# Decoder layer with grouped experts: the first blocks' preparations put in another order, and each expert's weights loaded in six pieces instead of three

## What is computed

```python
def expert_block(args):
    e, x_blk = args
    hidden = jax.nn.silu(x_blk @ exp_w_gate[e]) * (x_blk @ exp_w_up[e])
    return hidden @ exp_w_down[e]
...
x = x + hybrid_mixer(h, w_in[l], ..., w_out[l])
h = rmsnorm(x, ln2_g[l])
x = x + hierarchical_moe(h, ...)      # 32 experts, 2 for each token
return rmsnorm(x, ln_f_g)
```

## Time and profile before

| what | value |
|---|---|
| times of three runs | 1393.38, 1395.4, 1390.2 us; median 1393.38 |
| the profiled execution's own time | 1391.23 us |
| its span (first to last instruction) | 1389.6 us |
| PE busy | 1217.4 us, 88% |
| DVE busy | 884.1 us, 64% |
| ACT busy | 737.6 us, 53% |
| HBM read, written | 245.52 MB, 25.79 MB |
| `mix_and_route` ends, `experts` begins | about 726 us |
| `experts` ends, `finish` begins | about 1364 us |

### The profile page before, as it was taken

How to read it: one execution, slowest core, us unless ns; L and a number is a source line. 1 busy time by engine, 2 the same in 40 slices (tenths; PEclk the granted TensorE clock), 3 DMA queues, 4 the chain that set the end, 5 groups by cost and what they waited for, 6 DMA issues and landing times. The chain is left out here.

```text
span 1389.6 us, 17581 instructions
## 1 busy us (share of the span) xinstructions
PE 1217.4 (88%) x6516; PEld 949.5 (68%) x6516; DVE 884.1 (64%) x823; ACT 737.6 (53%) x756; POOL 269.6 (19%) x268
## 2 busy tenths in 40 slices
PE   3999999898899988699935999999999999999990
PEld 2867677676688768388824777777777777777760
DVE  5155554646366348334566788888888888887853
ACT  6154545545343243312224777776778777677643
POOL 0000000000201002000063343343333243233330
PEclk9999999999999995599967999999999999999995
DMA  5210101000111020163219899999999999999927
GB/s 166 61 31 16 31 16 31 15 17 1 46 46 31 1 90 32 46 234 121 92 42 372 308 366 369 362 355 359 364 358 360 365 359 354 359 351 354 358 70 265
DMA packets 69807, 263.22 MB, mean 189 GB/s; under 512 B 12944, under 2 KB 46848, under 8 KB 57472
## 3 DMA queue, kind: packets, MB, share of 16 engines
q1 hardware_dynamic: 60880, 245.69, 47.8%
q0 software_dynamic: 8880, 16.88, 5.3%
HBM read 245.52 MB, written 25.79 MB: 195 GB/s over the span
## 5 line engine op out<-in xcount | busy, mean ns | idle before, releaser
L1814 PE MATMUL ps<-w_high,x_hi 128*128 128x512 f32 x512 | 206.7, 404 | 3.3 <-DVE x_lo L1735 3.3
L1814 PE MATMUL ps<-w_high,x_lo 128*128 128x512 f32 x512 | 203.7, 398 | 0.0
L1814 PE MATMUL ps<-w_lower,x_hi 128*128 128x512 f32 x512 | 203.5, 397 | 0.0
L1731 DVE TENSOR_TENSOR w_lower<-w_raw,w_high 128x2048 fp32r<-128x2048 f32 x64 | 143.7, 2287 | 45.0 <-ACT w_high L1660 45.0
L1660 ACT ACTIVATE w_high<-w_raw 128x2048 fp32r<-128x2048 f32 x62 | 115.8, 1908 | 85.9 <-DMA w_raw<-exp_w_up 82.0
L1726 DVE TENSOR_TENSOR w_lower<-w_raw,w_high 128x2048 fp32r<-128x2048 f32 x62 | 141.6, 2284 | 24.7 <-ACT w_high L1654 24.7
L1590 POOL DMA_INDIRECT y_dram<-y,where x32 | 86.6, 2706 | 359.4 <-ACT y L1685 359.4
L1754 DVE TENSOR_TENSOR d_lo<-cat,d_hi 128x2048 fp32r<-128x2048 f32 x64 | 145.1, 2284 | 17.5 <-ACT d_hi L1675 17.4
L420 DVE TENSOR_TENSOR_SCAN prod<-stay 128x256 f32<-128x256 f32 (+7 forms) x64 | 83.4, 1345 | 91.0 <-ACT beta L371 91.0
L1654 ACT ACTIVATE w_high<-w_raw 128x2048 fp32r<-128x2048 f32 x62 | 118.5, 1911 | 40.7 <-DMA w_raw<-exp_w_gate 39.3
L1675 ACT ACTIVATE d_hi<-cat 128x2048 fp32r<-128x2048 f32 x64 | 122.0, 1907 | 6.8 <-PE ps L1841 6.6
(11 more groups left out here) (252 smaller groups left out, 2274.3 us busy)
## 6 DMA issues: line engine op xcount, KB each, us to landing
w_raw<-exp_w_gate SPq DMA_DIRECT2D x32, 2048.0 KB, 11.0
w_raw<-exp_w_up SPq DMA_DIRECT2D x32, 2048.0 KB, 12.4
cat<-exp_w_down SPq DMA_DIRECT2D x32, 2048.0 KB, 14.1
w_raw<-w_in SPq DMA_DIRECT2D x25, 512.0 KB, 3.8
xt<-x SPq DMA_DIRECT2D x8, 512.0 KB, 7.5
w_raw<-w_out SPq DMA_DIRECT2D x8, 512.0 KB, 5.3
x_g<-x SPq DMA_DIRECT2D x8, 512.0 KB, 3.8
y_dram<-cat SPq DMA_DIRECT2D x8, 512.0 KB, 4.8
```

What stands on the lines that cost most here:

```text
L1731: dve.tensor_tensor(u_lo[:, part], w_u[:, part], u_hi[:, part].bitcast(F32), ALU.subtract).then_inc(ulo, 1)
L1814: mm = pe.matmul(out, x_[:, n // 3, :], w_[:, n // 3, :], start=(n == 0), stop=(n == 3 * KD - 1))
```

## The change

What it does, in four parts.

1. The four primes are issued on POOL in `mix_and_route`, ahead of the scatters of the token lists. POOL in `experts` then begins with the third gather.
2. The down weights of block 0 are loaded by SP in `mix_and_route`, after the last tile of `h2` has been sent out and before the load of the lists; in `experts` ACT splits them first of all, and DVE splits them before the gate weights of block 1. ACT's `x_split(1, 1)` comes ahead of `g_split(1, 0)`, and DVE's `u_split(0, 0)` ahead of `x_split(0, 0)`.
3. SP's loads at the start of `experts` come in the order gate 1, up 1, down 1 (before: gate 1, down 0, up 1, down 1).
4. Each load of weights is two DMAs of 1 MB instead of one of 2 MB. Each half has a semaphore of its own, is issued as soon as that half of the tile is free, and ACT's split of a half waits for that half alone.

```diff
@@ mix_and_route, SyncE's queue
+                for m in range(2):
+                    part = slice(4 * m, 4 * m + 4)
+                    sp.dma_start(tile[:, part], dram_[0].rearrange("(p k) n -> p k n", p=P)[:, part]).then_inc(landed[m], 16)
...
+            sp.wait_ge(x1_out, 16 * NT)
+            sp.wait_ge(turned, 2 * NT)
+            sp.wait_ge(ss_done, NT)
+            for m in range(2):
+                part = slice(KF // 2 * m, KF // 2 * (m + 1))
+                sp.dma_start(w_d[0][:, part], a["exp_w_down"][0][0].rearrange("(p k) n -> p k n", p=P)[:, part])\
+                  .then_inc(d_in[0][m], 16)
             sp.wait_ge(listed, 16 * 2 * NT)
             sp.dma_start(lists[0:CAP, 0:EXPERTS, :], by_position(k)[0:CAP]).then_inc(lists_in, 16)
...
@@ mix_and_route, GpSimd
             pool.wait_ge(blanked, 16)
+            for j in range(2):
+                for landed in (scattered[j], more_in[j]):
+                    pool.dma_start(nothing[:], k["slots"][SLOT_ROWS - 1:SLOT_ROWS, :]).then_inc(landed, 16)
+                    pool.wait_ge(landed, 16)
...
@@ experts, SyncE's queue
             for j in range(2):
                 sp.wait_ge(gathered[j], 16)
-            sp.wait_ge(glo, 2)
-            load(sp, w_g, wg, 1, g_in)
-            down(0, 0)
-            sp.wait_ge(ulo, 2)
-            load(sp, w_u, wu, 1, u_in)
-            down(1, 1)
+            for m in range(2):
+                sp.wait_ge(glo, m + 1)
+                load(sp, w_g, wg, 1, g_in, m)
+            for m in range(2):
+                sp.wait_ge(ulo, m + 1)
+                load(sp, w_u, wu, 1, u_in, m)
+            for m in range(2):
+                down(1, 1, m)
...
-                    sp.wait_ge(glo, 2 * b + 4)
-                    load(sp, w_g, wg, e2, g_in)
-                    sp.wait_ge(dlo, 2 * b + 2)
-                    down(j, e2)
-                    sp.wait_ge(ulo, 2 * b + 4)
-                    load(sp, w_u, wu, e2, u_in)
+                    for m in range(2):
+                        sp.wait_ge(glo, 2 * b + m + 3)
+                        load(sp, w_g, wg, e2, g_in, m)
+                    for m in range(2):
+                        sp.wait_ge(dlo, 2 * b + m + 1)
+                        down(j, e2, m)
+                    for m in range(2):
+                        sp.wait_ge(ulo, 2 * b + m + 3)
+                        load(sp, w_u, wu, e2, u_in, m)
...
@@ experts, ScalarE
             def g_split(b, m, first=False):
-                act.wait_ge(g_in, 16 * b + 16)
+                act.wait_ge(g_in[m], 16 * b + 16)
...
+            d_split(0, 0, 16, 0, True)
+            d_split(0, 0, 16, 1, True)
             act.wait_ge(made, MADE)
             x_split(0, 0)
+            x_split(1, 1)
             g_split(1, 0)
             sigmoid(0)
             g_split(1, 1)
-            x_split(1, 1)
-            d_split(0, 0, 16, 0, True)
-            d_split(0, 0, 16, 1, True)
             u_split(1, 0)
...
@@ experts, VectorE
+            u_split(0, 0)
             x_split(0, 0)
+            u_split(0, 1)
             for m in range(2):
-                u_split(0, m)
+                d_split(0, 0, m)
+            x_split(1, 1)
             g_split(1, 0)
             gate_mul(0)
             g_split(1, 1)
-            x_split(1, 1)
-            for m in range(2):
-                d_split(0, 0, m)
```

More of the change, by code:

```diff
@@ L175, in _build @@
         with ExitStack() as c:
-            tiles = expert_tiles(k, c, raw, high, lower)
+            tiles = expert_tiles(k, c, cat, raw, high, lower)
             with ExitStack() as c2:
@@ L1073, in _, with expert_tiles @@
                 sums(1, h)
-def expert_tiles(k, c, raw, high, lower):
+def expert_tiles(k, c, cat, raw, high, lower):
     sb, sem, a = k["sb"], k["sem"], k["a"]
@@ L1082, in expert_tiles @@
     for n, (x, name) in enumerate((("g", "gate"), ("u", "up"))):
-        w[x] = (raw[:, n], a[f"exp_w_{name}"][0], sem(f"e_{x}_in"))
+        w[x] = (raw[:, n], a[f"exp_w_{name}"][0], [sem(f"e_{x}_in{m}") for m in range(2)])
         parts[x] = (high[:, n], lower[:, n], sem(f"e_{x}hi"), sem(f"e_{x}lo"))
@@ L1088, in expert_tiles @@
     who_made, gathered = sem("e_who"), [sem(f"e_gathered{j}") for j in range(2)]
-    return w, parts, x_g, who, lists, who_made, gathered
+    w_d, d_in = [cat[:, KF * j:KF * (j + 1), :] for j in range(2)], [[sem(f"e_d_in{j}{m}") for m in range(2)] for j in range(2)]
+    scattered, more_in = ([sem(f"e_{n}{j}") for j in range(2)] for n in ("scattered", "more"))
+    nothing = sb("nothing", [1, 4], F32, c)
+    return w, parts, x_g, who, lists, who_made, gathered, (w_d, d_in, scattered, more_in, nothing)
 def by_position(k):
@@ L1115, in mix_and_route @@
     halves = sb("halves", [P, 2], I32, out_c)
-    weights, parts, x, who, lists, who_made, gathered = tiles
+    weights, parts, x, who, lists, who_made, gathered, (w_d, d_in, scattered, more_in, nothing) = tiles
     (w_g, wg_dram, g_in), (w_u, wu_dram, u_in) = weights["g"], weights["u"]
@@ L1197, in _ @@
                 sp.wait_ge(wolo, 4 * n + 4)
-                sp.dma_start(tile[:], dram_[0].rearrange("(p k) n -> p k n", p=P)).then_inc(landed, 16)
+                for m in range(2):
+                    part = slice(4 * m, 4 * m + 4)
+                    sp.dma_start(tile[:, part], dram_[0].rearrange("(p k) n -> p k n", p=P)[:, part]).then_inc(landed[m], 16)
             for t in range(NT):
@@ L1261, in split @@
             def split(tile, hi, landed, done, m):
-                act.wait_ge(landed, 16)
+                act.wait_ge(landed[m], 16)
                 act.activation(hi[:, 4 * m:4 * m + 4], tile[:, 4 * m:4 * m + 4], ACT.Copy).then_inc(done, 1)
@@ L1524, in experts @@
     block_e, block_row, halves = tables
-    weights, parts, x_g, who, lists, who_made, gathered = tiles
+    weights, parts, x_g, who, lists, who_made, gathered, (w_d, d_in, scattered, more_in, nothing) = tiles
     (w_g, wg, g_in), (w_u, wu, u_in) = weights["g"], weights["u"]
-    wd, d_in = k["a"]["exp_w_down"][0], [sem(f"e_d_in{m}") for m in range(2)]
+    wd = k["a"]["exp_w_down"][0]
     HF = KF // 2
-    w_d = [cat[:, KF * j:KF * (j + 1), :] for j in range(2)]
     d_hi, d_lo = (sb(n, [P, KF, D], F32R, c) for n in ("d_hi", "d_lo"))
@@ L1534, in experts @@
     weight = [sb(f"weight{j}", [P, 1], F32, c) for j in range(2)]
-    nothing = sb("nothing", [1, 4], F32, c)
     x_hi, x_lo = ([sb(f"{n}{j}", [P, KD, P], F32R, c) for j in range(2)] for n in ("x_hi", "x_lo"))
@@ L1538, in experts @@
     y = [sb(f"y{j}", [P, D], F32, c) for j in range(2)]
-    scattered, more_in = ([sem(f"e_{n}{j}") for j in range(2)] for n in ("scattered", "more"))
     where_made = sem("e_where")
@@ L1553, in turned_h, with load @@
         return bank(k, 7, KF * CAP).rearrange("p (k n) -> p k n", n=CAP)
-    def load(sp, tile, dram_, e, landed):
-        sp.dma_start(tile[:], dram_[bass.ds(e, 1)].rearrange("o (p k) n -> p (o k) n", p=P)).then_inc(landed, 16)
+    def load(sp, tile, dram_, e, landed, m):
+        part = slice(4 * m, 4 * m + 4)
+        sp.dma_start(tile[:, part], dram_[bass.ds(e, 1)].rearrange("o (p k) n -> p (o k) n", p=P)[:, part])\
+          .then_inc(landed[m], 16)
     with nc.Block(no_gpsimd_drain=True) as block:
@@ L1560, in _, with down @@
         def _(sp):
[L1561 to L1562 removed]
+            def down(j, e, m):
+                part = slice(HF * m, HF * (m + 1))
+                sp.dma_start(w_d[j][:, part], wd[bass.ds(e, 1)].rearrange("o (p k) n -> p (o k) n", p=P)[:, part])\
+                  .then_inc(d_in[j][m], 16)
             for j in range(2):
                 sp.wait_ge(gathered[j], 16)
[L1566 to L1571 removed]
+            for m in range(2):
[6 more added lines that the diff above has]
+                down(1, 1, m)
             n_less = sp.value_load(halves[0:1, 1:2], min_val=EXPERTS // 2 - 1, max_val=MAX_HALVES - 1)
@@ L1597, in name_places @@
                 pool.tensor_copy(weight[j][0:CAP, :], at[:, 0, 2:3]).then_inc(where_made, 1)
-            for j in range(2):
-                for landed in (scattered[j], more_in[j]):
-                    pool.dma_start(nothing[:], k["slots"][SLOT_ROWS - 1:SLOT_ROWS, :]).then_inc(landed, 16)
-                    pool.wait_ge(landed, 16)
             pool.wait_ge(gathered[0], 16)
@@ L1656, in u_split @@
             def u_split(b, m, first=False):
-                act.wait_ge(u_in, 16 * b + 16)
+                act.wait_ge(u_in[m], 16 * b + 16)
                 if not first:
```

5 lines of the change are left out of this document (1 added, 4 removed).

## The result

The changed kernel took 1374.59 us (median of 4 runs, 1372.48 to 1377.78) against 1391.79 us for the kernel before, run beside it: ratio 0.988, 95% interval 0.984 to 0.991. That is 17 us less where I had forecast 10; it lies inside the range of 1371 to 1394, near its lower end. Run once more among the experiments, the same program took 1374.98 us, ratio 0.987 (0.983 to 0.990). The profiled execution has a span of 1374.5 us against 1389.6.

The account below looks back on a forecast made before the run. The prediction took the DMA engines to bound the expert stage from about block 4, PE 6% behind. Its terms, 6 + 2 + (8 - 6) = 10 us, took the median from 1393.4 to 1383 us, range 1371 to 1394.

Parts of the forecast that it names:

- Parts 1 to 3: Expert stage's start: moved down load and primes, reordered first work save DMA time; 6 us, between 4 and 9.
- early down load: Block 0's down weights, moved into a hole before the expert stage: 4.9 us less 0.4 delay, net 4.5 us.
- The hole of the earlier trace: Idle DMA engines near 772 us after the third gather's stall: 4.5 us, forecast to become 3.6.
- The room that the pieces fill: Expert loop after 876 us: halves asked for sooner keep the queue seldom empty; gain 8 us, 0 to 10.4.
- The packets: All 31 blocks: 8 KB runs need twice the packets; cost 0.2 us a block, 6 us, 0 to 23.
- The last blocks: After up 30 lands, the first half is split while the second arrives; gain 2 us, 1 to 2.3.
- B: Rival, 0.15: packets cost nothing, the loop's whole 10.4 us room is taken, first blocks give 9; 1372 us.
- C: Rival, 0.20: loop gains nothing, 358 GB/s being what this mix reaches; only head and tail gain; 1385 to 1391 us.
- D: Rival, 0.15: packets cost 0.5 to 0.75 us a block; no gain from 0.52 on, 1400 us at 0.75.

Follow-up runs that it names:

- e1: The changed kernel with part 4 undone, weight loads whole again at 2 MB each; 1390.41 us, ratio to before 0.997.
- e9: The changed kernel with both pieces of a tile issued together once the whole tile is free, and ScalarE waiting for both before splitting; 1394.60 us, ratio 0.999.
- e2: The kernel before with part 4 alone, the rest as in before; 1373.65 us, ratio 0.987.
- e4: The changed kernel with block 0's down weights loaded in the expert stage again and ACT's and DVE's first work in the old order; 1379.42 us, ratio 0.991.
- e6: The changed kernel with both halves of a tile issued together once the whole tile is free, each half keeping its semaphore; 1378.09 us, ratio 0.988.
- e7: The changed kernel with halves issued early, but ScalarE waiting for both before it splits the first; 1374.68 us, ratio 0.986.
- e10: e9 with four transfers of 0.5 MB a tile and 4 KB packets; 1404.05 us, ratio 1.007.
- e11: e8 with each 1 MB piece as two transfers of 0.5 MB, 4 KB packets; 1379.52 us, ratio 0.989.
- e5: The changed kernel with block 1's down weights also loaded in routing's tail, behind the load of the lists; 1374.42 us, ratio 0.985.
- e3: The changed kernel with the primes in the expert stage again, ahead of the third gather; 1376.81 us, ratio 0.988.
- e8: The changed kernel with the primes behind the slot scatters, without waits between them, reading four bytes of `b_group` each; 1371.65 us, ratio 0.983.

## Why the prediction was right, and where it wasn't

The direction, the bound and the range held, and so did most of what was to show it: no wait for the third gather, transposes for block 2 at 761.68, which is 24.0 us behind the first gate load (forecast 755 - 731.5 = 23.5), a block in 413.0 / 22 = 18.8 us (18.9), a share of 1.00. A weight load took 404 x 0.888 x 2.097 / 135.94 = 5.53 us of queue 1 in the change, where I had 5.6. The kernel is bound by its DMA engines from block 8 or so on, and filling their idle time came through to the end. But the 17 us are made up otherwise than my 10. The steps from before to e1, to e9, to the change add up in the spans: +1.0, +4.0, -20.1. That the number came out inside the range owes something to luck: I gave 6 us to parts that brought nothing and nothing to a place where the pieces brought 6.8.

**Parts 1 to 3, forecast 6 (4 to 9): measured about nothing.** In the place that I looked at the sum was right: the first eight blocks of e1 take 149.2 us instead of 155.0, 5.8 less. What failed is that I gave no time to what lies ahead. The routing tail grew by 4.7 us, the way from `h_dram` to the first gate load by 1.1. I had allowed 0.4 for the latter; with the early down load it is 18.8 to 19.5 us (with 4 KB packets or a second such load 21.0 to 21.4), in the two kernels without it (e2, e4) 16.8 and 16.7. So that load costs about 2.4 us there and brings 5.8 in the blocks (e4): net 3.4 in the stretches and 4.8 in the medians, where I had 4.5. The hole of the earlier trace rows I had made smaller, from 4.5 to 3.6 us; e1 has it at 754 us, and 0.60 x 6 = 3.6 us it is, by chance, since I had worked it out for gate 2 asked for in halves:

```profile
754.00:760.00 6.00, 3.89 (x12) 3.05 (x13) 5.19 (x5) 5.99 (x5) 0.00 (x0) 0.78 0.40 141
```

In the change the same six microseconds have a share of 0.95, so 0.3 us. It is the early issue that fills the hole and not the pieces as such: with late issue it stays (0.60 from 754 to 760 in e9, 0.47 from 752 to 758 in e6), and in e7, early but joint, the shares from 746 to 758 are 0.96 and 0.93. In the sum of the 3.6 us each request's bytes begin 1.7 us after its issue (752.2 for 750.5); no run shows such a time. In the trace of before, SyncE asks for gate 3 at 775.45, and the DMA engines, at rest until then, are at work from about 776.0 on, 0.6 us later:

```profile
775.50:776.00 0.50, 0.50 (x4) 0.39 (x3) 0.50 (x1) 0.00 (x0) 0.00 (x0) 1.00 0.00 0
776.00:776.50 0.50, 0.50 (x4) 0.41 (x3) 0.50 (x1) 0.41 (x1) 0.00 (x0) 1.00 1.11 229
```

In the 22 blocks e1 lost 2.1 us to before, which I can't explain beyond the 1.1 us that two profiles of one program differ by.

**The room that the pieces fill, forecast 8 (0 to 10.4): measured 9.8 in the loop, and 6.8 more in the first eight blocks.** This is the term that was mis-sized. From e9 to the change the 22 blocks go from 422.8 to 413.0 us, which the share and the rate of the earlier trace rows had foretold. The error was to take this room from the window after 876 alone and to hold the blocks before it for PE-bound, since PE has no gap from 800 on in the earlier trace rows. That is true of before. In e9 the DMA queue is short of requests in the first eight blocks as it is later (147.9 against 141.1 us), and I had put nothing there. From 800 to 880 us, e9 and then the change:

```profile
800.00:880.00 80.00, 75.68 (x352) 57.99 (x350) 69.08 (x45) 59.94 (x46) 30.69 (x26) 1.00 0.97 354
800.00:880.00 80.00, 80.00 (x374) 61.99 (x373) 70.83 (x45) 63.16 (x46) 30.32 (x27) 1.00 1.01 372
```

So with the queue kept full PE runs without a gap up to 880 us, and into the DMA limit only behind that.

**The mechanism behind it was half told.** I wrote that a half is asked for sooner and the queue is seldom empty. Read from the first gate load to the end, it is 657.2 us with neither early issue nor use by halves, 643.6 with use by halves alone, 640.4 with early issue alone, and 636.4 with both. Each alone gives 13.6 or 16.8 of the 20.8 us; together they give not 30 but 20.8. Both shorten the same round: landed, split on ScalarE and VectorE, asked for again. Why one does so well for the other I read from that sum, from ScalarE's longest waits (4.4 us in e9, 2.5 in e6, 3.2 and 3.4 for up and gate in e7) and from the GB/s; how many bytes stood in the queue at each time I did not measure.

**The packets, forecast 6 (0 to 23): measured 3.7 from the first gate load to the end (e1 to e9), 4.2 in the medians.** That is 0.12 us a block for three more transfers and twice the packets, where I took 0.2. The two ratios to before, 0.997 and 0.999, lie 2.6 us apart with overlapping intervals, so this price is hardly clear of noise. Queue 1 took 404 x 0.860 x 2.097 / 132.16 = 5.51 us for a load with 8 KB packets (e9), the 5.51 that I find with 16 KB before the change (133.80 MB at 87.0%), and 404 x 0.869 x 2.097 / 130.26 = 5.65 us with 4 KB (e10). The price was the right thing to set against the pieces. The queue's own time shows it only from 8 to 4 KB; in the whole time it is 4.2 us for the first halving and 9.5 for the second, which adds twice as many packets (from 876 to 1280 us queue 1 has 9188 before, 18148 in e9, 35772 in e10), so that to scale it by packet count was not far off. The 4 KB stores of the earlier trace rows were too dear a row for it: 0.25 us more for a load, where e10 shows 0.14. The Trainium skill ("DMA: Bandwidth & Descriptors", section "Anatomy of one DMA") gives a DMA issued from GpSimd about 2.0 us beside its bytes; the weights are issued from SyncE. The trace agrees with the way I read it, that such a part is hidden while others stand in line, since three more transfers a block cost 0.12 us and not 6. The Trainium skill ("DMA: Bandwidth & Descriptors", section "Rules for kernel authors") wants at least 1 MiB in a DMA for the full bandwidth; e10 and e11, with 0.5 MB, are 9.5 and 7.9 us slower, so the trace agrees, though the size of the transfers and that of the packets were halved together and which of them costs is open.

**The last blocks, forecast 2 (1 to 2.3): measured 3 to 4.** From the last gate load to the end it is 82.0 and 82.3 us where a half is used as it lands (e6, change) and 85.6 and 86.5 where it isn't (e7, e9). In the profile of the change the two halves of up are split at 1313.14 and 1315.70, with the second piece landing behind the first one's split. ScalarE's rows:

```profile
1313.14 1.92 ACT L1677 ACTIVATE w_high<-w_raw 128x2048 fp32r<-128x2048 f32 x1 [0.71 <-DMA w_raw<-exp_w_up]
1315.70 1.92 ACT L1677 ACTIVATE w_high<-w_raw 128x2048 fp32r<-128x2048 f32 x1 [0.63 <-DMA w_raw<-exp_w_up]
```

VectorE's row:

```profile
1315.82 4.48 DVE L1748 TENSOR_TENSOR w_lower<-w_raw,w_high 128x2048 fp32r<-128x2048 f32 x2
```

From the second landing at 1315.70 to the end of VectorE's share at 1320.30 it is 4.6 us; I had 4.2. Against the 6.4 us of the earlier trace rows that is 1.8 less, so the other 1 to 2 us lie elsewhere in that stretch.

**Of the rivals,** B (1372) came nearest in the number, but not by its sum: it let the packets cost nothing and the first blocks give 9. C fell with 363 GB/s after 876 (364 in the repeat). The Trainium skill ("DMA: Bandwidth & Descriptors", section "Specifications") names a limit of about 358 for a core; it did not bind here. D's price shows one size further down, at 4 KB, but smaller: 9.5 / 31 = 0.31 us a block, where D needed 0.52.

**What stays open** is the routing tail. With the primes ahead of the scatters it is 19.2 to 20.4 us in six profiles (the change, its repeat, e1, e4, e9, e10) and 15.5 or 15.6 in three (e5, e6, e7); with the primes elsewhere it is never over 16.2 (before, e2, e3, e8, e11). The change and e6 differ only in SyncE's waits in the expert stage, which runs later. The change repeats its own value. VectorE's wait ahead of the last scores goes with it: 6.0 us in five of the six (4.6 in e1), 3.1 or 3.2 in e2, e3, e5, e6 and e7, 2.1 in before, e8 and e11. So it isn't what the primes do to the queue, at least not alone. That it hangs on how the program's code is laid out is a guess which no run here tests. If the 5 us of tail were gone, the change would stand near e8.

## What to carry to other kernels

Where single buffers feed a full DMA queue, shorten the round from landed to asked for again: ask for a half when it is free, or use a half when it has landed. Either alone gave most of it here (13.6 and 16.8 of 20.8 us), so don't add them up, and use by halves also shortens the very end. Where the first loads run out before the next one is asked for, only the early issue filled the hole. Look for the missing requests in every block and not only where PE shows gaps. Halve a transfer for this, but not twice: at 0.5 MB and 4 KB a packet the price was about half the gain, 9.5 of the 20 us between e9 and the change.

A gain summed in one stage should be read off in that stage, and the stages ahead of it too: here 5.8 us won in eight blocks were given back before the first of them began.

## What the runs showed of the hardware that I had not expected

With smaller packets from SyncE the indirect gathers behind them land sooner: in the same window the median of `x_g` from issue to landing is 14.6 us before the change, 14.1 in e1 (both 16 KB), 9.6 in e9 (8 KB) and 7.6 in e10 (4 KB). With the halves issued early and used singly it is 10.1 at 8 KB (the change) and 9.3 at 4 KB (e11), so the second step is small there. The Trainium skill ("DMA: Bandwidth & Descriptors", section "Queues, rings and completion order") says that an engine takes turns between its queues packet by packet, and that fits. In e9 and e10 no gain came of it; my reading is that the gathers are issued a block ahead. Where one is late it seems to be worth something: in e2 the third gather was issued at 749.04 and PE began on it at 758.96, 9.9 us later, against 765.65 - 752.14 = 13.5 before.

One wait of VectorE, ahead of the last scores, is 6.0 us in two executions of one program and 3.1 us in a program that differs from it only in SyncE's instructions of a later stage. The cause is open.
